# Two transformer blocks on one core: input projection in rounds, four projections split into rounded parts, and compressed attention started earlier

## Time and profile before

| what | value |
|---|---|
| median of 3 runs | 1657.17 us (1652.24 to 1659.6) |
| the profiled execution, own time | 1656.26 us |
| its span, first to last instruction | 1654.4 us |
| PE busy | 1556.4 us, 94% of the span |
| DVE, ACT, POOL busy | 1101.6, 840.4, 1103.9 us |
| mean granted PE clock | 0.977 |

### The profile page before, as it was taken

One profiled execution on the slowest core, in us unless ns is written; L12 is line 12 of the kernel. 1 busy time (PEld: TensorE's weight loads), 2 busy tenths in 40 slices (PEclk: granted clock), 3 DMA queues, 4 the chain that ended last, 5 costly groups with the idle time before them and its releaser, 6 DMA issues. The chain is left out here.

```text
span 1654.4 us, 27016 instructions
## 1 busy us (share of the span) xinstructions
PE 1556.4 (94%) x9679; PEld 1359.3 (82%) x9679; DVE 1101.6 (67%) x1666; ACT 840.4 (51%) x1437; POOL 1103.9 (67%) x453
## 2 busy tenths in 40 slices
PE   2898898999999999999999999999999988999999
PEld 2685537999999999988888888888888756799987
DVE  5563645999937777768888888761756275368850
ACT  1454215555566666655445554547764354554443
POOL 0771006889986666658888888855985621688896
PEclk9999789999999999999999999999999889999999
DMA  7665355455454444435555555545554510455554
GB/s 278 207 230 203 127 181 201 165 178 178 153 190 141 140 141 141 141 127 190 190 194 193 196 190 191 198 141 176 192 192 140 166 52 26 153 179 182 187 179 140
DMA packets 77397, 280.07 MB, mean 169 GB/s; under 512 B 8577, under 2 KB 9089, under 8 KB 77186
## 3 DMA queue, kind: packets, MB, share of 16 engines
q1 hardware_dynamic: 76592, 276.68, 49.3%
q10 hardware_dynamic: 722, 2.27, 0.4%
HBM read 277.86 MB, written 1.05 MB: 169 GB/s over the span
## 5 line engine op out<-in xcount | busy, mean ns | idle before, releaser
L2071 POOL TENSOR_TENSOR low<-ring,high 128x1024 fp32r<-128x1024 f32 x449 | 1103.7, 2470 | 539.9 <-ACT high L977 539.3
L977 ACT ACTIVATE high<-ring 128x1024 fp32r<-128x1024 f32 x449 | 472.8, 1058 | 438.1 <-PE PS L346 381.7
L344 PE MATMUL PS<-hTh,high 128*128 128x256 f32 (+1 forms) x1648 | 472.7, 287 | 9.7 <-POOL low L2071 7.5
L346 PE MATMUL PS<-hTh,low 128*128 128x256 f32 (+1 forms) x1648 | 467.9, 284 | 0.0
L345 PE MATMUL PS<-hTl,high 128*128 128x256 f32 (+1 forms) x1648 | 467.8, 284 | 0.0
L344 PE MATMUL PS<-high,hTh 128*128 128x512 f32 x940 | 370.6, 394 | 14.4 <-POOL low L2071 5.9
L345 PE MATMUL PS<-low,hTh 128*128 128x512 f32 x940 | 367.9, 391 | 0.0
L346 PE MATMUL PS<-high,hTl 128*128 128x512 f32 x940 | 367.8, 391 | 0.0
L1801 DVE TENSOR_TENSOR hTl<-region,hTh 128x256 fp32r<-128x256 f32 x128 | 289.2, 2261 | 57.9 <-ACT hTh L1231 57.9
L344 PEld LDWEIGHTS PS<-hTh,high 128*128 128x128 f32 (+1 forms) x1648 | 316.3, 192 | 13.0 <-POOL low L2071 9.2
L345 PEld LDWEIGHTS PS<-hTl,high 128*128 128x128 f32 (+1 forms) x1648 | 316.2, 192 | 0.0
(11 more groups left out here) (283 smaller groups left out, 1535.1 us busy)
## 6 DMA issues: line engine op xcount, KB each, us to landing
ring<-in_stream SPq DMA_DIRECT2D x523, 512.0 KB, 3.3
X<-in_x SPq DMA_DIRECT2D x1, 1024.0 KB, 5.1
region<-in_band ACTq DMA_DIRECT2D x1, 1024.0 KB
result<-X SPq DMA_DIRECT2D x4, 256.0 KB, 2.0
region<-in_skeys ACTq DMA_DIRECT2D x1, 512.0 KB
region<-in_consts ACTq DMA_DIRECT2D x1, 352.0 KB, 3.4
region<-in_wpool ACTq DMA_DIRECT2D x1, 256.0 KB
cols<-in_cols SPq DMA_DIRECT2D x1, 208.0 KB, 5.1
```

The lines of the kernel that those rows point to most:

```text
L344: pe.matmul(out_, sh, mh, start=start, stop=False, **kw)
L346: return pe.matmul(out_, sl, mh, start=False, stop=stop, **kw)
L977: act.activation(high[:, b % RING, :], ring[:, b % RING, :], ACT.Copy).then_inc(rounded[b % RING], 1)
L2071: pool.tensor_tensor(low[:, b % RING, :], ring[:, b % RING, :], high[:, b % RING, :].bitcast(F32), ALU.subtract).then_inc(left[b % RING], 1)
```

## The change

Six edits.

1. Order of the stream: the 16 quarters of ada0 to ada3 no longer come first as a whole. After ada_j (4 quarters) come quarter j of in1, in0 and in2. The columns of `w_ada` are rearranged so that ada_j holds scale and shift of feature chunks 2j and 2j+1. PE, DVE and ACT run four rounds: sum ada_j, shift and split two chunks, multiply one quarter of three blocks.
2. ada6 is paired with in4, not with in1; DVE does it between `qk1_normed` and the index scores. PE's `turned1(5..7)` come after the first half of z1(3).
3. `up_pool`, `up_attn`, `out0`, `out1` are split, and so are their inputs (poolT by ACT and POOL, the attention output and the turned M1 by ACT and DVE into hTh and hTl). ACT rounds the four quarters of up_attn inside the last four steps of attention a1.
4. `high` and `low` slots are counted over split quarters only (`part`), not over all.
5. Second block: ACT writes the doubled compressed inputs directly while it evicts z2(2) (DVE's 8 copies go); of the selected and window keys DVE writes one copy (4 instructions in place of 8), ACT the second, after z2(6).
6. `RO_PARTS` becomes tiles 0-2, 3-5, 6, 7-10, so that L923 has four tiles behind it; the waits for `PZT` and `rec_gated` and the compressed values of tile 0 move into units 0 and 1 of attention a2.

```diff
-PAIRED = {"in1": "ada6", "in6": "ada7", ...
+HEAD = ("in1", "in0", "in2")
+PAIRED = {"in4": "ada6", "in6": "ada7", ...
 def quarter_no(name, q):
+    if name in ORDER[0:QUARTERS]:
+        return (QUARTERS + len(HEAD)) * ORDER.index(name) + q
+    if name in HEAD:
+        return (QUARTERS + len(HEAD)) * q + QUARTERS + HEAD.index(name)
-SPLIT = [... in ("in", "pq", ...
+SPLIT = [... in ("in", "up_pool", "up_attn", "out", "pq", ...
+SPLIT_NO = [0] + np.cumsum(SPLIT).tolist()
+def part(b):
+    return SPLIT_NO[b] % RING
...
 # PE
+            turn_pair(0)
+            for j in range(QUARTERS):
                 wait_used(pe, f"ada{j}")
                 ada(j)
+                for name in HEAD:
+                    z1(int(name[2:]), (j,))
+                if j + 1 < QUARTERS:
+                    turn_pair(j + 1)      # waits norm_shifted of j, uses bank 3
+            z1(3, (0, 1))
             turned1(5, Z); turned1(6, Z)
             pe.wait_ge(sem("ik1_normed"), 1)
             turned1(7, N1).then_inc(sem("ik1_turned"), 1)
-            z1(3)
+            z1(3, (2, 3))
...
+            pe.wait_ge(sem("pool_split"), 1)
-            pe.wait_ge(sem("attn1_kept"), 2)
+            pe.wait_ge(sem("attn1_split"), 2)
-            pe.wait_ge(sem("turned_kept"), kept_by("m1", KC))
-            transposes("c2", N2, "n2_filled", 2)
+            transposes("c2", XN2, "z2_kept", 2 * 3)
-            transposes("k2", N2, "n2_filled", 3)
+            transposes("k2", N2, "k2_doubled", 2 * T)
-            RO_PARTS = (range(0, 3), range(3, 6), range(6, 9), range(9, RT_N))
+            RO_PARTS = (range(0, 3), range(3, 6), range(6, 7), range(7, RT_N))
-            pe.wait_ge(sem("turned_kept"), kept_by("pz", KC))
-            pe.wait_ge(sem("rec_gated"), 4)
-            cmp_values(0)
 # PE, attention
+                    if tag == "a2" and u < 2:     # wait for the half of PZT in the banks of unit u
+                        ...
+                    if tag == "a2" and u == 1:
+                        pe.wait_ge(sem("rec_gated"), 4)
+                        cmp_values(0)
...
 # ACT
+            for j in range(KC // 2):
+                ahead(HEAD[0], j, 0)
+                act.wait_ge(sem("norm_shifted"), nth_norm("n1", KC // 2, j + 1))
+                act.activation(hTh[:, 2 * j:2 * j + 2, :], normed1[:, 2 * j:2 * j + 2, :], ACT.Copy)...
+                ahead(HEAD[2], j, 0)
 # ACT, attention
+                    if tag == "a1" and u >= n - 2:
+                        ahead("up_attn", u - (n - 2), 0)
 # ACT, up_pool: poolT rounded ahead of z1(6)
+            ahead("up_pool", 1, 0)            # then the sigmoids, then the other two quarters
-            wait_used(act, "up_pool")
+            wait_product("up_pool")
 # ACT, out
+            ahead("out0", 1, 0)
+            mixed_high("m1")
+            ahead("out0", 2, 0)
             act.wait_ge(sem("ada_summed"), 8)
...
+            ahead("out1", 1, 0)
             for i in range(2):                # gate1, waits for ada sums 4 and 5
...
+            ahead("out1", 3, 0)
 # ACT, keys of the second block, after z2(6)
+            for w in range(2):
+                for t in range(T):
+                    act.wait_ge(sem("n2_filled"), 1 + 2 * w + t + 1)
+                    act.activation(both[:, :, 1, :], both[:, :, 0, :], ACT.Copy)...
 # DVE
+            for j in range(KC // 2):
+                ada(j)
+                dve.wait_ge(sem("ada_summed"), j + 1)
+                ...  # bias, 1 + scale, two shifted chunks, wait for hTh, hTl
-            ada(6)
...
             normed1_heads(slice(0, 9), 3, ..., "qk1_normed")
+            ada(6)
...
 # POOL
+                if b == quarter_no("up_pool", 0):
+                    pool.wait_ge(sem("pool_rounded"), 1)
+                    pool.tensor_tensor(low_, poolT..., high_..., ALU.subtract)...
```

More of the change, by code:

```diff
@@ L85 @@
 NCOL = _at
-PAIRED = {"in1": "ada6", "in6": "ada7", "up_pool": "ada8", "out0": "ada5", "out1": "ada10",
+HEAD = ("in1", "in0", "in2")
+PAIRED = {"in4": "ada6", "in6": "ada7", "up_pool": "ada8", "out0": "ada5", "out1": "ada10",
           "pq1": "ada11"}
 def plan():
-    order = [f"ada{j}" for j in range(4)]
-    for name in [f"in{i}" for i in range(Z1B)] + ["up_pool", "ada9", "ada4", "up_attn", "out0", "out1", "pq0", "pq1"]:
+    order = [f"ada{j}" for j in range(4)] + list(HEAD)
+    for name in [f"in{i}" for i in range(len(HEAD), Z1B)] + ["up_pool", "ada9", "ada4", "up_attn", "out0", "out1", "pq0", "pq1"]:
         order += [name] + [PAIRED[n] for n in [name] if n in PAIRED]
@@ L336, in parts @@
         def parts(b):
-            return Pair((high[:, b % RING, :], low[:, b % RING, :]))
+            return Pair((high[:, part(b), :], low[:, part(b), :]))
         def product(pe, out_, stat, mov, start, stop, **kw):
@@ L715, in _ @@
                 ada(j)
-            out1(2, 3, done="out1_done")
+            out1(2, 3, done=True)
             norm_transposes("n2", XN1)
@@ L975, in round_quarter @@
                 if nth_split(b) > 1:
[L976 to L978 removed]
+                    act.wait_ge(multiplied[part(b)], nth_split(b) - 1 + r)
+                act.activation(high[:, part(b), :], ring[:, b % RING, :],
+                               ACT.Copy).then_inc(rounded[part(b)], 1)
             def ahead(name, q=QUARTERS - 1, n=RING - 1):
@@ L2068, in lower_quarter @@
             def lower_quarter(b, r=0):
-                pool.wait_ge(rounded[b % RING], nth_split(b) + r)
-                pool.tensor_tensor(low[:, b % RING, :], ring[:, b % RING, :], high[:, b % RING, :].bitcast(F32),
+                pool.wait_ge(rounded[part(b)], nth_split(b) + r)
+                pool.tensor_tensor(low[:, part(b), :], ring[:, b % RING, :], high[:, part(b), :].bitcast(F32),
                                    ALU.subtract).then_inc(left[b % RING], 1)
             first, last = START["u0"], START["rx"]
-            for b in range(START["in0"], first):
+            for b in range(first):
+                if b == quarter_no("up_pool", 0):
+                    high_, low_ = tuple(pool_parts)
+                    pool.wait_ge(sem("pool_rounded"), 1)
+                    pool.tensor_tensor(low_, poolT.rearrange("p g s -> p (g s)"), high_.bitcast(F32),
+                                       ALU.subtract).then_inc(sem("pool_split"), 1)
                 if SPLIT[b]:
```

226 lines of the change are left out of this document (132 added, 94 removed).

## The result

The changed kernel takes 1663.7 us (median of 13 runs, 1658.6 to 1668.6) where the kernel before takes 1653.8 beside it; ratio 1.0064, 95% interval 1.0046 to 1.0083. Run again unchanged in another session: 1663.2, ratio 1.0074 (1.0054 to 1.0095). So it is 9 to 12 us slower (by the medians 9 to 10, by the ratios 11 to 12), where I had forecast 5 faster. That 1663.7 still lies just inside the range's end of 1664 is luck: that end was built from the bounds of rounds, ada6 and attention, and the term that overshot most, out, wasn't among them. Its profiled run took 1665.4, of which 1663.6 are the span.

What follows compares the result with a forecast made beforehand. PE, busy for 94% of the span, was taken as the bound, so only its own work and gaps count. The terms summed to -5.2 us, from 1656.3 to 1651.1, with a range of 1636 to 1664.

Steps and rivals of the forecast that it cites:

- Rounds: Input projection at the start: four rounds of about 15.2 us end at 80.5 instead of 84.2, -3.7 us.
- ada6 and turned1: Between in2's end and the index scores: ada6's later place makes the scores late for PE, +4.0 us, between 0 and +7.
- in5, in6, up_pool: Stall in in6 goes, -0.9 us; split up_pool waits for late roundings, +0.7, bounds -3.4 and +2.
- Attention and up_attn: Attention a1 held by POOL's remainders, up_attn shorter by 3.5 us; together +2.0, bounds -2.7 and +4.
- out0, out1: Output projection: shorter split products -6.3 us, late roundings at out1's end +5.1; net -1.2, bounds -5 and +3.
- Keys and compressed logits: Second block: PE's wait at the keys goes, -2.4 us; gaps at the compressed logits go, -3.7, bounds -2.5 and -5.4.
- the first block keeps its gain: Rival, first block: rounds -6, ada6 0, out -4 among its terms; -21 us in all, 1635; chance 0.28.
- The clock stays low in the rounds: Rival, rounds at the start: each round's 8.2 us take 16.4, 26 us more in all, 1677; chance 0.11.

Runs made afterwards that it cites:

- e13: Kernel before plus the second block's edits and the rounds, with ada's biased sums kept in PSUM for the two-column instruction: 1647.7 us, ratio 0.9967.
- e15: Kernel before plus second block's edits, rounds with biased sums in PSUM, ada6 behind up_pool, out split with roundings ahead of gate1: 1648.5 us, ratio 0.9971.
- e14: Kernel before plus the second block's edits and the rounds, with ada6 put behind up_pool and DVE's ada(6) behind ada(8): 1647.8 us, ratio 0.9978.
- e9: The changed kernel, unchanged, run and profiled once more: 1663.2 us, ratio 1.0074.
- e7: The changed kernel with up_attn as one plain fp32 product again, its quarters neither rounded nor lowered: 1663.4 us, ratio 1.0065.
- e3: The changed kernel with DVE's 22 small decay instructions moved from between attention a1 and M1 to behind ada(10): 1664.2 us, ratio 1.0057.
- e4: The changed kernel with ScalarE's rounding of out1's last two quarters put ahead of its gate1 copies: 1658.9 us, ratio 1.0035.
- e1: The kernel before with only the change's edits behind the recurrent block (the second block): 1643.4 us, ratio 0.9928.

## Why the prediction was wrong, by its steps

**Rounds** (-3.7). In the profile of after -3.4. By the means in2 ends at 83.2 us with the old head (six kernels) and 83.5 with rounds (nine executions), so there is no gain. A round of 15.2 was right as the undisturbed case: in e13 and e15, where the small instruction isn't held, rounds follow each other by 14.5 to 16.1, 15.4 in the mean. The step counted two held 512-column instructions of DVE a round and left out the two-column one, though L1580 stood in the earlier trace rows with its 1.20: once out of the pause I took it as gone for good. It costs up to 2.0 in one to three of the four rounds.

**ada6 and turned1** (+4.0; measured +8.4, bound +7). e14 puts 6.3 of it on ada6's place in the ring; that the other 2 belong to turned1's place is argued, not shown. The chain of norms, ada(6) and scores is as told, but PE's path isn't: I had it wait for the scores, with in4's last quarter 1.2 late on the way; it waited 1.32 and 3.35 for in4's quarters and 0.19 for the scores. Mis-sized: the norms that ada(6) waits behind took 4.83, held too, and I had taken the 2.66 of the earlier trace rows.

**in5, in6, up_pool** (-0.2; measured +0.3). Right to half a microsecond in this profile, which is luck: the ten executions with up_pool split take 29.3 to 31.9, 30.3 in the mean, so +1.2. The stall of 0.94 in in6 did go: with up_pool plain and the slots counted by `part`, five kernels take 27.7 to 28.9, 28.0 in the mean. So the split itself costs 2.3, where I had +0.7. What varies is the split up_pool: in after PE did its first half at the low clock, 7.38 us, which hid most of ScalarE's sigmoids (wait 1.19); in e9 it did it in 5.82 and then waited 2.73.

**Attention and up_attn** (+2.0; measured +3.3). Right in mechanism: e7 shows the two sides in its profile, +6.9 and -3.6, where I had +5.5 and -3.5; its runs show no gain.

**out0, out1** (-1.2; measured +8.2 with the tiny sums). This is the step that failed: "The rounding of M1 hides behind the 32 tiny sums of 4.3 us that stand there anyway". It asked what hides the rounding, and not when M1 itself is ready. I had moved DVE 4.5 to 6.4 us later a paragraph above, and up_attn's end 3.5 nearer to its start, and carried neither to the next work in DVE's queue, the 22 small instructions with their 6.15 us of slack. Against up_attn's end DVE lost 10.3: 2.7 in the attention, 3.3 by the shorter up_attn, 4.3 by the two held instructions. e3 shows the delay of M1 gone when they stand elsewhere, and e7 when DVE isn't late and GpSimd is idle. Of the 6.6 us some 2.5 are PE's longer wait and 4.1 the low clock behind it; e9 had the wait without the low clock, and there the step cost 2.2. Five profiles with the 22 instructions in their place and up_attn split give 8.8 to 13.4 for the stage, 6.7 before. The +5.1 at out1's end was right in its cause (e4) and measured +5.9, and the products' part measured -4.2, predicted -6.3.

**Keys and compressed logits** (-2.4 and -3.7; measured -2.6 and -5.5). Right in mechanism; both lie beyond their bounds by 0.1, and the second was sized at two thirds of what came (-5.8 in e1). e1 shows 8.5 us in place and 12 in the runs.

The rival "the first block keeps its gain" failed in its largest terms: its -6 for the rounds came out at none by the means, its -4 for out at +8.2. "The clock stays low in the rounds" did not come: from 24 to 70 us 0.87 was granted. Each round did begin low, with records of 0.63 us for 3.1, 5.3, 3.3 and 4.0 us, where I had counted 3.2.

The Trainium skill, SBUF — State Buffer, section "SBUF: two separate sides", gives the lock to whichever starts first "for the whole instruction". The traces agree, down to two columns (2.15 instead of 0.16). By that rule size is no protection, which is what I should have taken from it.

## What to carry to other kernels

When a change puts work on one engine and makes another late, go through the late engine's queue until an engine that sets the end waits for it: the slack of each step is used once. Where GpSimd and DVE share a stretch, count for each GpSimd instruction that falls on the critical chain one DVE instruction held for up to its whole length, however small it is (two of 22 here, in each of five profiles), or keep one of the inputs in PSUM. And a block prefetched through a shared ring needs its reader to be free when it lands, or it stops the blocks behind it.

## What the runs showed of the hardware

A DVE TENSOR_SCALAR of 126 x 11 with one input, in SBUF, was held as well: 2.38 us instead of 0.17, begun 0.04 us after a GpSimd remainder (rows above). Moving the biased sums to PSUM removed the hold of a two-input instruction: 0.16 in all four rounds of e13, in three of which it began inside a remainder.

One program's profiles differ by several us in single stages (M1 and sums 8.9 and 13.4; 96 products 22.1 and 23.7), while its medians agree within 0.5 us. The granted clock behind a short wait is one cause (0.50 and 0.94 behind M1). A stage read off one profile is known no better than that.
